# Scores taken map by map, some decay distances on VectorE, and two weight pieces moved, in a fused attention and recurrence layer

## The reference

```python
# attention, per head: two score maps m of 64 columns each, a softmax of each, and their difference
scores = einsum(q[:, m], k[:, m]) * SCALE - slope * distance     # masked by blocks of 64 frames
p = softmax(scores);  a = p[0] - lam * p[1];  out = a @ v
# recurrence, per head, in chunks: state 128x128
cum = cumsum(log_f)
o = sum_{s<=t} exp(cum[t] - cum[s]) * q[t] * k[s] * v[s]  +  (q * exp(cum)) @ state
state = exp(cum[last]) * state + (k * exp(cum[last] - cum)) @ v
# then both are normalised, multiplied by silu(gate), projected by w_out, added to x and normalised
```

## Time and profile before

| what | value |
|---|---|
| median of three runs | 1533.54 us (1533.01 to 1533.68) |
| the profiled execution | 1533.85 us, its span 1532.1 us |
| granted TensorE clock, mean | 0.992 |
| TensorE busy | 1478.3 us (96%) |
| ScalarE busy | 966.7 us (63%) |
| VectorE busy | 876.6 us (57%) |
| GpSimd busy | 765.7 us (50%) |

### The profile page before, as it was taken

The page is one execution under the profiler, slowest core; times in us unless marked ns, Lnnn a source line. Parts: engine busy times, 40 slices in busy tenths (PEclk is TensorE's granted clock), DMA queues, the critical chain, the costliest instruction groups (busy, mean ns, idle before and its releaser), DMA issues.

```text
span 1532.1 us, 26281 instructions
## 1 busy us (share of the span) xinstructions
PE 1478.3 (96%) x8156; PEld 1250.0 (82%) x8156; DVE 876.6 (57%) x2469; ACT 966.7 (63%) x2602; POOL 765.7 (50%) x1819
## 2 busy tenths in 40 slices
PE   5999999999999999999999999999999999899997
PEld 4788888878888888878888888778888888788886
DVE  5466666675555666575555666754555566632332
ACT  6777777787666666786666666866666767511111
POOL 7655665556545655575546655665554335400000
PEclk9999999999999999999999999999999999999999
DMA  8554333252442212114422212124322221244332
GB/s 263 162 166 155 124 125 114 73 145 74 144 141 71 71 67 70 43 66 145 128 86 70 69 67 69 65 65 141 128 70 69 70 68 40 82 143 146 123 123 68
DMA packets 100288, 157.31 MB, mean 103 GB/s; under 512 B 8576, under 2 KB 78592, under 8 KB 91456
## 3 DMA queue, kind: packets, MB, share of 16 engines
q1 hardware_dynamic: 100160, 155.75, 31.1%
HBM read 111.16 MB, written 44.56 MB: 102 GB/s over the span
## 4 chain that ended last, share of the span: by engine, by line
PE 82%; DVE 8%; ACT 3%; issue 3%; POOL 2%; SPq 1%; DMA 1%; DVEq 0%; POOLq 0%; ACTq 0%
PE pab L571 38%; PE qkb L691 8%; PE oar L641 8%; PE qkb L755 6%; PE pab L755 6%; PE qkb L598 4%; PE tb L632 4%; DVE scores L1176 2%; DVE masked L1107 1%; DVE kq L1206 1%; PE qkb L594 1%; PE oar L614 1%; PE tb L742 1%; PE oar L611 1%; PE oar L613 1%
## 5 line engine op out<-in xcount | busy, mean ns | idle before, releaser
L571 PE MATMUL pab<-w_hi,xr 128*128 128x512 f32 x2176 | 783.6, 403 | 10.1 <-DVE w_lo L1037 8.5
L571 PEld LDWEIGHTS pab<-w_hi,xr 128*128 128x128 f32 x2176 | 412.7, 190 | 90.4 <-issue 8.5
L571 PE MATMUL pab<-w_lo,xr 128*128 128x512 f32 x1088 | 427.2, 393 | 0.0
L1408 POOL TENSOR_TENSOR dd<-dd 128x64 f32<-128x64 f32 x340 | 103.9, 306 | 366.6 <-DVE dd L1159 366.3
L571 PEld LDWEIGHTS pab<-w_lo,xr 128*128 128x128 f32 x1088 | 207.0, 190 | 33.5
L1127 DVE TENSOR_TENSOR q<-tb,q 64x128 fp32r<-64x128 f32 x136 | 39.3, 289 | 287.9 <-ACT kp L901 287.0
L691 PE MATMUL qkb<-kp,q 128*128 128x512 f32 (+3 forms) x656 | 186.0, 365 | 8.1 <-DVE mxs L1176 6.4
L921 ACT ACTIVATE scores<-scores,nmx 128x128 f32<-128x128 f32 (+16 forms) x136 | 156.6, 1160 | 17.4 <-DVE nmx L1186 17.4
L691 PEld LDWEIGHTS qkb<-kp,q 128*128 128x128 f32 x656 | 118.5, 188 | 48.7 <-issue 16.3
L861 ACT ACTIVATE fb<-pab,nrs 128x256 f32<-128x256 f32 x68 | 32.3, 475 | 198.7 <-PE pab L571 198.6
L641 PE MATMUL oar<-vv,at 128*128 128x128 f32 x1104 | 152.4, 277 | 0.0
(11 more groups left out here) (161 smaller groups left out, 2834.3 us busy)
## 6 DMA issues: line engine op xcount, KB each, us to landing
xr<-xs SPq DMA_DIRECT2D x51, 1024.0 KB, 5.2
xs<-xr SPq DMA_DIRECT2D x17, 1024.0 KB, 5.0
w_raw<-in_w_in SPq DMA_DIRECT2D x48, 256.0 KB, 6.1
w_raw<-in_x_turned SPq DMA_DIRECT2D x17, 512.0 KB, 4.9
mix<-mx SPq DMA_DIRECT2D x68, 128.0 KB, 2.2
xr<-mix SPq DMA_DIRECT2D x17, 512.0 KB, 5.4
w_raw<-in_x_prompt SPq DMA_DIRECT2D x16, 512.0 KB, 4.2
scores<-in_x_prompt SPq DMA_DIRECT2D x16, 512.0 KB, 4.8
```

Source lines behind the costliest of these rows:

```text
L571: last = mm(pab[:, b, :], x, w[:, kt, 512 * b:512 * b + 512], start=(kt == 0 and part == 0 and w is w_hi), stop=(kt == KT - 1 and part == 1))
L1408: g.tensor_tensor(o[:, :, 0, :], ref, c[:, :, 0, :], sub)
```

## The change

1. Score units go map by map: all chunks of map 0, then all of map 1 (before: both maps of a chunk, then the next chunk). Each map has its own negated maximum and signal, and ScalarE takes each exponential apart: map 0 ahead of `recurrence_columns`, map 1 behind it.
2. With four or six units TensorE starts them one step later (after kt = 3); `transpose_recurrence` stands two steps earlier (b = 0, kt = 4).
3. VectorE: in every tile with one chunk `apply_decay` comes ahead of the scores (before: behind `finish`, but for SAMPLE); with more chunks `finish` stands behind the second unit and `apply_decay` behind the fourth, as before, but a map's negated maximum comes as soon as its last chunk is read.
4. Five of the 13 distance subtractions (two widest levels and that to the tile's end) go from GpSimd to VectorE, right behind the running sum; ScalarE's L930 waits for both engines.
5. Last tile of a head: ScalarE has pieces 0 to 4 of the next weights, exponential 0, piece 5, `recurrence_columns`, exponential 1, `copy_recurrence`, pieces 6 and 7.

```diff
@@ project (TensorE)
-                after = 2 if len(units) > 2 else 4
+                after = {2: 4, 4: 3, 6: 3}.get(len(units), 2)
...
-                    if b == 0 and kt == 6:
+                    if b == 0 and kt == 4:
                         transpose_recurrence(h, t, first)
...
             def qk_units(t):
-                return [(c, m) for c in range(len(chunks_of(t))) for m in range(2)]
+                return [(c, m) for m in range(2) for c in range(len(chunks_of(t)))]
@@ ScalarE
-            def softmax_exp(h, t):
+            def softmax_exp(h, t, m):
                 n = keys_of(t)[1]
-                need(act, h, "neg_max", t + 1)
-                for m in range(2):
-                    last = F(scores[:, m, 0:n], scores[:, m, 0:n], ACT.Exp, bias=nmx[:, m:m + 1], scale=SCALE,
-                             accum_out=sums[:, m:m + 1])
-                last.then_inc(S["prob_ready"], 1)
+                need(act, h, "neg_max", 2 * t + m + 1)
+                F(scores[:, m, 0:n], scores[:, m, 0:n], ACT.Exp, bias=nmx[:, m:m + 1], scale=SCALE,
+                  accum_out=sums[:, m:m + 1]).then_inc(S["prob_ready"], 1)
...
                     if t == SAMPLE:
-                        split_weights(h, 1, range(6))
+                        split_weights(h, 1, range(5))
+                    if before:
+                        softmax_exp(*before, 0)
+                    if t == SAMPLE:
+                        split_weights(h, 1, (5,))
                     recurrence_columns(h, t)
-                    if t == SAMPLE:
-                        split_weights(h, 1, (6, 7))
                     if before:
-                        softmax_exp(*before)
+                        softmax_exp(*before, 1)
...
                     copy_recurrence(h, t)
                     if t == SAMPLE:
+                        split_weights(h, 1, (6, 7))
                         split_weights(h, 0, (0, 1))
@@ VectorE, behind the running sum
+                need(dve, h, "cum_ready", t + 1)
+                n = P if t < PT else DEC
+                cum = dd[:, NX - 1, :]
+                for j in WIDE:
...
+                    tt(o[:, :, 0, :], ref, c[:, :, 0, :], ALU.subtract)
+                    tt(o[:, :, 1, :], c[:, :, 1, :], ref, ALU.subtract)
+                tt(dd[:, 0, 0:n], cum[:, n - 1:n].to_broadcast([P, n]), cum[:, 0:n], ALU.subtract
+                   ).then_inc(S["dist_wide"], 1)
@@ biased_scores (VectorE)
-                if t == SAMPLE:
+                if len(chunks) == 1:
                     apply_decay(h, t)
...
+                for i, (m, c) in enumerate((m, c) for m in range(2) for c in range(len(chunks))):
...
+                    if c > 0:
+                        need(dve, h, "qk_free", u)
...
+                    if c == len(chunks) - 1:
+                        need(dve, h, "qk_free", u + 1)
+                        ts(nmx[:, m:m + 1], mxs[:, m, c:c + 1], -SCALE, None, ALU.mult).then_inc(S["neg_max"], 1)
+                    if i == 1 and len(chunks) > 1:
                         finish(*before)
-                    if c == 1:
+                    if i == 3:
                         apply_decay(h, t)
```

More of the change, by code:

```diff
@@ L44 @@
 NX = NS + 2
+WIDE = (0, 1)
 HP = P // 2
@@ L284, in build @@
                 t_use["cache", t] = len(t_use)
-            for c in range(len(chunks_of(t))):
-                for m in range(2):
+            for m in range(2):
+                for c in range(len(chunks_of(t))):
                     qk_use["qk", t, c, m] = len(qk_use)
                     qk_index[t, c, m] = len(qk_index)
+            for c in range(len(chunks_of(t))):
                 at_index[t, c] = len(at_index)
@@ L994, in _ @@
                 head(h, False)
-            softmax_exp(HEADS - 1, SAMPLE)
+            for m in range(2):
+                softmax_exp(HEADS - 1, SAMPLE, m)
             epi_hi(0, 1)
```

46 lines of the change are left out of this document (21 added, 25 removed).

## The result

The changed kernel is slower. Its median is 1537.01 us (8 runs, 1534.91 to 1538.14) against 1533.32 us of the kernel before in the same comparison; the ratio is 1.0027, with a 95% interval of 1.0016 to 1.0038. The forecast was 1522 us, so it was wrong in sign, by 15 us. The profiled execution took 1537.65 us with a span of 1535.9 us; that is 3.8 us above the span before, and the granted clock is the same (0.993, before 0.992).

What follows compares the result with a forecast made beforehand. TensorE, busy 96% of the span, bounds the kernel, so only its waits and half-clock stretches can be won. Terms -8 - 4 + 6 - 2 - 3.6 = -11.6 from 1533.85 us gave 1522 us, range 1511 to 1532.

Steps and rivals of the forecast that it cites:

- long tiles: 12 tiles with four chunks: keys start sooner, later chunks wait for reads; -0.2 us each, -2, bounds +2 and -6.
- middle tiles: 32 tiles with two or three chunks: new waits +10.4 us, first-unit waits gone -4.4; net +6, bounds -4 and +16.
- Short tiles: One-chunk tiles: decayed keys ahead of scores remove 15 waits on `kq`; -8 us, bounds -4 and -9.
- Start: Head 0's start: queries' wait and half clock go, 6.2 us; earlier transposes cost +2; -4 together, bounds 0 and -5.
- Distances: Five subtractions per tile moved to VectorE, 1.3 us, costed at nothing in 68 tiles because VectorE would otherwise wait there.
- no wait on `nb` but the first: Sign of being right: TensorE waits for `nb` only at its first use, no size given.
- Rival 4: ScalarE held ahead of `recurrence_columns` by map 0's maximum and exponential, delaying `nb` in 32 tiles; 1541 us, chance 0.09.
- Last tiles: Each head's last tile: later pieces 6 and 7 free 1.7 us, half taken; -0.9 in four heads, -3.6, bounds 0, -7.
- Rival 2: Short tiles wait for GpSimd in place of VectorE; 1533 us, or about 1530 without the last tile term; chance 0.17.

Runs made afterwards that it cites:

- e1: Kernel before with one part alone, decayed keys (apply_decay) ahead of the scores in one-chunk tiles: 1525.20 us against 1532.78 for the kernel before.
- e6: Changed kernel with all 13 distance subtractions on GpSimd again: 1540.03 us against 1531.82 for the kernel before.
- e3: Changed kernel with each chunk's maximum started from the chunk two before, so no read waits for the one just before: 1528.04 us against 1532.78 before.
- e9: Changed kernel with four and six score units starting after kt = 2, as in the kernel before: 1528.43 us against 1531.51 before.
- e12: Changed kernel with the edits of e3 and e9 together: 1526.24 us against 1531.73 for the kernel before.
- e2: Changed kernel with the transposes of `nb` back at b = 0, kt = 6: 1534.96 us against 1532.78 for the kernel before.
- e7: Changed kernel with GpSimd's last two remainders (pieces 6 and 7) only after `combine` of the last tile: 1534.62 us against 1531.82 before.

## Why the prediction was wrong

The steps that failed are two terms of the sum: the price of a read that waits for the read just before it (long tiles, -0.2 each), and the lateness of the keys in the middle tiles, taken from the later units without that wait (+6). The runs show +3.5 and +10.0 us in their place. By parts:

- **Short tiles: right in kind, the size partly by luck.** -8 was forecast, -7.1 measured, and e1 shows that the order on VectorE makes it. But the forecast counted 12 waits in heads 1 to 3, 6.1 us by its prices, and three in head 0; heads 1 to 3 won 7.3, and head 0 nothing (+0.3, and +1.2 in e1), though its three waits of 1.1 us went. In its tile 2 a new wait of 0.56 us for `nb` came; the rest stays open.
- **Start: right.** +2.5 in tile 0 for the +2 of the forecast, -5.9 in tile 1 for -6.2, closer than the 1.5 us by which kernels with the same start differ, so the fit proves little.
- **Distances: right.** e6 shows nothing in tiles 5 to 15; a gain of some 2 us in head 0's short tiles and the first tiles was not credited.
- **Middle tiles: right in kind, wrong in size.** +6 was forecast (+10.4 of waits, -4.4 of first units that no longer wait), +10.0 measured: 6.0 in the tiles with two chunks and 4.1 in those with three. Three chunks came about as worked out (4.8 us of waits), by the fifth read. Tile 8 came within what was worked out (0.4 to 0.8 us; 0.55 idle and some 0.16 beyond it), but by two errors that cancel in part: the keys ran at 1.08 us, for which the working gives 0.4, and the reads were later than worked out. The mean of the 16 tiles with two chunks is 0.37 us after what the first units save, where 0.35 was taken ahead of it. The step that failed is the length of the row of reads ahead of the keys: "starts 0.69 later ... ends at 809.71, a maximum lies between" counts the later units alone. The wait of a read for the read just before it is named by the prediction, but under the long tiles only; it stands in every tile with more than one chunk. e3 takes it away and gives back 6.8 of the 10.0 us; e9 takes away the later start and gives back 8.3; e12 takes away both and gives back 9.8. So each uses up the same spare time ahead of L596. The later start alone (e3) costs 3.2 us and the chain alone (e9) 1.7, the two together 10.0.
- **Long tiles: wrong in sign.** "each later chunk now waits for the read just before it. I take -0.2 each, -2": the wait was seen and given no price of its own (and 12 times 0.2 would be 2.4). It adds 0.25 to 0.33 us from read to read (0.86 and 0.94 for 0.61 us), and the seventh and eighth units wait for such reads: 18 bank waits in these tiles for 11 before, none in e3. Measured were +3.5 us, and -1.8 with the chain gone (e3): the forecast holds for the kernel without it. This is the largest error of the sum, 5.5 us.
- **First tiles: left out of the sum.** +1.9 us in three heads. The text named "no wait on `nb` but the first" as a sign of being right; there were four more, 2.0 us together, three of them in first tiles and one in tile 2 of head 0. e2 shows that the earlier transposes make them. Rival 4, ScalarE held ahead of the columns in 32 tiles, did not come: no tile behind a head's third waits for `nb`. In tile 13 of head 2 ScalarE does begin the columns 1.1 us later, close to the 1.2 worked out, but `nb` is still done 1.7 us before TensorE asks.
- **Last tiles: right in kind.** -0.9 each was forecast, -0.7 measured in heads 0 to 2. e7 shows that `combine` beside the two remainders keeps back another 0.8 us each; so half the price was near, but half was taken without a working, and its fit is luck.

In sum the middle tiles missed by 4.0, the long tiles by 5.5, the first tiles by 1.9, the last tiles with the end by 2.6, short tiles and start by 1.4: 15.4 us between the forecast of -11.6 and the 3.8 us measured. Of the last 2.6, 1.1 lie in the end, which varies by more. Rival 2 did not come, no short tile waits for GpSimd; its sum also put the upper end of the middle tiles at 5 us above the forecast, where the bound of +16 lies 10 above. Rival 4 was the only slower case that I had, and its place was wrong; the slower case that came true was the sum of two of my own terms taken too small.

## What to carry to other kernels

A value handed from one instruction to the very next on the same engine can be a wait (0.17 to 0.18 us here), also where no other engine is in it: when a loop is turned round so that a running maximum passes between neighbours, price that gap once per pair, in every tile that has pairs. Two small delays on one chain ahead of the same consumer are not priced apart: find the consumer's spare time first (here 0.07 us in tile 8), and ask which of them would fit. And before an instruction is moved behind others, follow its signal into the DMA queue: what is issued behind it there can hold another engine a tile later.

## What the runs showed of the hardware

- A score read on VectorE that takes its start value from the read just before starts 0.17 to 0.18 us after that one's end and takes 0.75 us; one with a constant takes 0.68 us and can start 0.61 us after the start of the one ahead, as that one's accumulator is read out (826.55 and 827.16 in tile 9 of head 2 of the changed kernel). The Trainium skill (VectorE: DVE Perf Modes, The DRAIN you can't avoid) says that a one-column statistic used as the next instruction's scalar is read stale without a semaphore, and also that a semaphore after each instruction cost nothing in its measurement. No run here shows a stale read, and none repeats that measurement, which was of copies. A wait on the instruction just ahead, for its value, has a price here: with it it is 0.86 to 0.94 us from read to read, without it 0.61, and 0.07 of the difference is the longer read.
- Exclusion between VectorE and GpSimd has a size here: 2.74 against 4.79 us for four instructions of 128x512. Whether a kernel gains by it depends on what the blocked instruction was: in e3 it was the small one ahead of `combine` (1.34 us for 0.22, the row below), and the last tile of head 2 took 26.42 us for 25.38, although `combine` was done equally late in both (21.8 us into the tile), since in the changed kernel its first part was out before the remainders held it.

```profile
980.02 1.34 DVE L1214 SCALAR_TENSOR_TENSOR cneg<-sums,rsum,lam 128x1 f32<-128x1 f32 x1
```
